# The passage from W_o to the FFN rebuilt around two cross sums, and the result of a decoder layer put together in token rows

## The chip, the cores and the metric

One core of a Trainium2 chip runs the kernel. The metric is the device time of one execution in microseconds. TensorE multiplies matrices, VectorE and ScalarE do everything element by element, GpSimd does little here, and SyncE (SP) issues most DMAs. Matrices in fp32 are multiplied as three products of high and low halves.

## The reference

One step of a decoder layer for 256 prompt tokens and 8 x 4 sample tokens, 288 in all, D = 2048, all fp32. The attention and the gated convolution ahead of it, and the caches, are not touched. What matters is this end of the layer:

```python
def _rmsnorm(x, g):
    y = x * lax.rsqrt(jnp.mean(x * x, axis=-1, keepdims=True) + RMS_EPS)
    return y * g

    m = (sigmoid(ga) * a + sigmoid(gb) * b) @ w_o
    x = x + gate1 * _rmsnorm(m, g_post1)                    # x1
    h = _rmsnorm(x, g_pre2) * (1.0 + scale2) + shift2       # h2
    g, u = jnp.split(h @ w_ffn_in, 2, axis=-1)              # 2 x 5632 columns
    f = (jax.nn.silu(g) * u) @ w_ffn_out
    return x + gate2 * _rmsnorm(f, g_post2)
```

shift, scale and gate come from silu(c) @ w_ada + b_ada, one set for the prompt and one for each of the eight sample sequences.

## The kernel before

**Layout.** Features lie on the 128 partitions and tokens in the columns: xT, r_T, a_hi, a_lo, x1A, f_T are 16 feature tiles (kt) of 288 columns, the first 256 prompt, the last 32 samples. All products put weights on the stationary side and 288 token columns on the moving side.

**Products.** A weight block of 512 x 512 (1 MB) is loaded by SP into one of four raw slots (load_w), ScalarE rounds it to w_hi (split_hi), VectorE forms w_lo (split_lo), each into one of two buffers. TensorE's product(n, ...) then does 4 output tiles (mt) x 4 feature tiles x 3 matmuls. ScalarE may overwrite a buffer when the product that used it is done, so both splits of block n+1 happen while product n runs. The order of each engine's work is written out by hand; semaphores carry the dependences (raw_turn: w_lo is made; mm_turn: groups of a product are done; bank_turn: PSUM banks are evicted; act_hi, act_lo: halves of the input are made).

**W_o stage.** Four turns (o_turn) of four products. After a turn, gated() on ScalarE squares each output tile into sq4 and evicts it times gate1·g_post1 into r_T; VectorE adds the squares (add_square) into sqr. Beside the products TensorE works through the remaining columns of w_ada in groups of 512 (ADA): four slots of fp32 matmuls (ada_slot), ScalarE copies the group (copy_ada), TensorE turns it (ada_transpose), VectorE adds the four parts (add_ada). Groups ADA_T and ADA_T + 1 are done in the passage.

**Passage.** sum_partitions adds sqr and the last square over partitions, as a product with ones into bank 7. inverse_root makes rstd with logarithm and exponential on ScalarE and one refining step in three VectorE operations (refine_root). add_normed scales r_T by rstd and adds it to xT, in 8 pieces of two tiles: xT is now x1. ScalarE squares each piece (square_x1), TensorE sums the squares over partitions, and ScalarE scales x1 into x1A (scale_x1). A second inverse_root follows, then h2 = x1A·rstd + shift2 piece by piece (h2_times_rstd, split_h2, h2_lo). TensorE meanwhile does the two ADA groups, and eight matmuls into bank 6 whose result nothing reads. The first FFN product waits for pieces 0 and 1; pieces 2 to 7 are made in the first FFN turn ahead of the product that needs them. A turn of the FFN (f1_turn) is 4 products for the gate half, then 4 for the up half.

**End.** After W_ffn_out, r and x change roles with f: root, add_normed(f_T) into xT, TensorE turns each block of four tiles and 128 tokens (12 blocks, the third of each four with 32 tokens), ScalarE copies it to y_rows (one block VectorE), and SP stores four chunks of 512 columns.

## Time and profile before

| | |
|---|---|
| median of 3 runs | 1817.82 us (1817.79 to 1817.87) |
| profiled execution | 1817.98 us |
| its span | 1816.1 us |
| TensorE busy | 1792.5 us, 99% |
| VectorE busy | 887.6 us, 49% |
| ScalarE busy | 708.4 us, 39% |
| granted TensorE clock, mean | 0.997 |

The span runs from the first to the last instruction or transfer of the profiled execution; its own time is 1.9 us longer. Busy time of TensorE counts a matmul until its modelled end. A group's idle time says what ended the wait in front of it.

### The profile page before, as it was taken

The numbers are of one execution on the slowest core, as the hardware profiler recorded it, in microseconds if no ns is written. First come the engines' busy times: TensorE is split into PE (matmuls) and PEld (weight loads), VectorE is DVE, ScalarE is ACT, GpSimd is POOL, SyncE is SP. The second block draws the span as 40 slices with busy tenths as digits, with TensorE's granted clock in tenths as the row PEclk, the third lists the DMA queues.
The fourth block names the chain that finished last, engine by engine and source line by source line (L and its number), as shares of the span: only waits on it lengthen the run. The fifth ranks groups of instructions, "written<-read, shape, count | busy, mean of one in ns | idle before, by whom it ended". The sixth has DMA issues, their size and how long they took to land.

```text
span 1816.1 us, 31913 instructions
## 1 busy us (share of the span) xinstructions
PE 1792.5 (99%) x13683; PEld 1680.2 (93%) x13683; DVE 887.6 (49%) x1092; ACT 708.4 (39%) x829; POOL 23.7 (1%) x72
## 2 busy tenths in 40 slices
PE   9999999999999999999999999999999999999997
PEld 6888888897699999998969999999999999999996
DVE  3566662335644344453475344434444445565565
ACT  4433233335643333344363323333333334545453
POOL 0000100001000000000000000000000000000000
PEclk9999999999999999999999999999999999999999
DMA  9998788966655555559837555555555445555541
GB/s 322 380 361 310 266 302 303 339 240 210 243 186 168 168 165 166 162 203 349 305 118 255 192 201 163 164 165 168 168 166 163 162 162 162 163 164 164 168 156 52
DMA packets 193897, 382.38 MB, mean 211 GB/s; under 512 B 8998, under 2 KB 17662, under 8 KB 193504
## 3 DMA queue, kind: packets, MB, share of 16 engines
q1 hardware_dynamic: 190048, 378.04, 61.0%
q0 software_dynamic: 1328, 2.58, 0.4%
q8 instruction: 74, 1.21, 0.3%
q10 hardware_dynamic: 2424, 0.37, 0.2%
q14 instruction: 23, 0.18, 0.0%
HBM read 376.15 MB, written 4.81 MB: 210 GB/s over the span
## 4 chain that ended last, share of the span: by engine, by line
PE 94%; DVE 2%; ACT 1%; DMA 1%; SPq 1%; issue 1%; DVEq 0%; ACTq 0%
PE bank L621 29%; PE bank L623 28%; PE bank L622 28%; PE bank L631 4%; DMA ada<-in_w_ada 1%; PE bank L858 1%; PE bank L988 1%; PE bank L640 1%; PE bank L957 0%; SPq L455 0%; SPq L440 0%; DVE xT L2184 0%; PE bank L927 0%; DVE f_T L2176 0%; ACT x1A L1523 0%
## 5 line engine op out<-in xcount | busy, mean ns | idle before, releaser
L621 PE MATMUL bank<-a_lo,w_hi 128*128 128x288 f32 x3648 | 1085.1, 297 | 2.9 <-DVE a_lo L2194 1.5
L622 PE MATMUL bank<-a_hi,w_hi 128*128 128x288 f32 x3648 | 1076.2, 295 | 0.0
L623 PE MATMUL bank<-a_hi,w_lo 128*128 128x288 f32 x3648 | 1072.5, 294 | 0.0
L1612 DVE TENSOR_TENSOR w_lo<-raw,w_hi 128x2048 fp32r<-128x2048 f32 x240 | 550.0, 2292 | 700.9 <-ACT w_hi L1157 700.5
L1157 ACT CAST w_hi<-raw 128x2048 fp32r<-128x2048 f32 x239 | 455.9, 1907 | 854.6 <-PE bank L623 821.9
L621 PEld LDWEIGHTS bank<-a_lo,w_hi 128*128 128x128 f32 x3648 | 683.5, 187 | 22.1 <-issue 19.2
L623 PEld LDWEIGHTS bank<-a_hi,w_lo 128*128 128x128 f32 x3648 | 687.1, 188 | 0.0
L622 PEld LDWEIGHTS bank<-a_hi,w_hi 128*128 128x128 f32 x3648 | 684.9, 188 | 0.0
L631 PE MATMUL bank<-ada,cT 128*32 128x512 f32 (+1 forms) x608 | 64.5, 564 | 1.7 <-DMA ada<-in_w_ada 1.6
L1712 DVE TENSOR_TENSOR a_lo<-hid,a_hi 128x1152 fp32r<-128x1152 f32 x44 | 59.4, 1352 | 12.3 <-ACT a_hi L1187 12.3
L1187 ACT CAST a_hi<-hid 128x1152 fp32r<-128x1152 f32 x44 | 50.7, 1154 | 0.0
L631 PEld LDWEIGHTS bank<-ada,cT 128*32 128x32 f32 x608 | 17.9, 112 | 35.2 <-issue 29.9
L1697 DVE TENSOR_REDUCE mods<-bank 128x36 f32<-128x144 f32 (+1 forms) x22 | 6.7, 306 | 74.4 <-PE bank L640 74.3
L621 PE MATMUL bank<-o_lo,w_hi 128*128 128x288 f32 x128 | 37.9, 296 | 0.0
L621 PE MATMUL bank<-y_lo,w_hi 128*128 128x288 f32 x128 | 37.9, 296 | 0.0
L622 PE MATMUL bank<-o_hi,w_hi 128*128 128x288 f32 x128 | 37.8, 295 | 0.0
L622 PE MATMUL bank<-y_hi,w_hi 128*128 128x288 f32 x128 | 37.8, 295 | 0.0
L623 PE MATMUL bank<-o_hi,w_lo 128*128 128x288 f32 x128 | 37.6, 294 | 0.0
L623 PE MATMUL bank<-y_hi,w_lo 128*128 128x288 f32 x128 | 37.6, 294 | 0.0
L1561 ACT ACTIVATE sg<-bank 128x288 f32<-128x288 f32 x44 | 18.0, 408 | 36.8 <-PE bank L623 36.8
L1183 ACT COPY ada_sb<-bank 128x512 f32<-128x512 f32 (+1 forms) x26 | 14.4, 554 | 40.2 <-PE bank L631 40.2
L2247 DVE TENSOR_TENSOR sg<-bank,sg 128x288 f32<-128x288 f32 x44 | 19.0, 452 | 15.4 <-ACT sg L1561 15.4
(298 smaller groups left out, 943.7 us busy)
## 6 DMA issues: line engine op xcount, KB each, us to landing
raw<-in_w_ffn_in SPq DMA_DIRECT2D x88, 1024.0 KB, 5.1
raw<-in_w_in SPq DMA_DIRECT2D x75, 1024.0 KB, 10.6
ada<-in_w_ada SPq DMA_DIRECT2D x60, 1024.0 KB, 9.6
raw<-in_w_ffn_out SPq DMA_DIRECT2D x44, 1024.0 KB, 5.2
ada_o<-in_w_ada SPq DMA_DIRECT2D x26, 1024.0 KB, 9.6
raw<-in_w_o SPq DMA_DIRECT2D x16, 1024.0 KB, 6.1
ada<-in_w_ada SPq DMA_DIRECT2D x16, 512.0 KB, 10.2
raw<-in_cache_k SPq DMA_DIRECT2D x16, 512.0 KB, 4.3
```

Source lines behind the costliest of these rows:

```text
L621: pe.matmul(acc, w_hi[buf][:, a, cols], lo[:, kt, :], start=first and a == 0, stop=False)
L622: pe.matmul(acc, w_hi[buf][:, a, cols], hi[:, kt, :], start=False, stop=False)
L623: mm = pe.matmul(acc, w_lo[buf][:, a, cols], hi[:, kt, :], start=False, stop=last and a == tiles - 1)
L631: mm = pe.matmul(bank[4][32 * a:32 * a + 32, 0:cols.stop - cols.start], cT[:, SK * q + a, :], ring[q % len(ring)][:, a, cols], start=q == ...
L640: mm = pe.transpose(bank[5][:, m * P:m * P + P], ada_sb[:, m * P:m * P + P], ident[:, :])
L858: mm = pe.transpose(bank[4 + n % 2][:, f * P:f * P + P], raw[2 * j][:, n, f * P:f * P + P], ident[:, :])
L988: mm = pe.matmul(acc, lhs, rhs, start=blk == 0, stop=blk == 2, tile_position=(0, 32 * c), skip_group_check=True)
L1157: nc.scalar.copy(w_hi[buf][:, :, :], raw[s][:, :, :]).then_inc(hi_done, 1)
L1187: nc.scalar.copy(dst[:, kd:kd + tiles, :], src[:, bass.ds(kt, tiles), :]).then_inc(act_hi, 1)
L1612: tt(w_lo[buf][:, :, :], raw[s][:, :, :], w_hi[buf][:, :, :].bitcast(F32), ALU.subtract).then_inc(raw_turn, 1)
L1712: tt(lo[:, kd:kd + SK, :], src[:, bass.ds(kt, SK), :], hi[:, kd:kd + SK, :].bitcast(F32), ALU.subtract).then_inc(act_lo, 1)
L2247: tt(sg[:, mt, :], bank[mt][:, 0:NT], sg[:, mt, :], ALU.mult).then_inc(bank_turn, 1)
```

## The change

- **Sums.** With r the gated output of W_o and s = rstd, x1 = x + s·r, so the sum of x1² is x·x + 2s·(x·r) + s²·(r·r). The sum of x·x is taken from the first normalisation (its sums lie in small[:, 12:15]); VectorE spreads it on three diagonals (diag2), TensorE turns it into all partitions between the mixer and the W_o stage, and VectorE keeps it as base_x. VectorE forms x·r and r·r for the tiles of the first three W_o turns in the turn behind (cross_c, cross_q, into c_sum and q_sum), and tile by tile in the last (c_last, q_last, whose prompt columns ScalarE squares). TensorE sums both over partitions in ten matmuls ahead of group ADA_T. second_root puts the three together; rstd1 is a tile of its own.
- **x1 in pieces.** Pieces 0 and 1 are made before the FFN, the other six in the first FFN turn (x1_pieces). The square sums over x1 and the eight matmuls into bank 6 are gone.
- **First FFN turn.** Gate and up halves alternate for each group of four feature tiles, in banks 0 to 3 and 4 to 7, and the first product starts with piece 0 alone. Weight block N_F1 + 1 is rounded before the second root. The sigmoids move from the fourth product to the seventh.
- **ADA slots.** Two of the four slots of group ADA_T + 1 get another place and are loaded as soon as W_o is done.
- **End.** The sums of f² are made with tokens on partitions (one column for each 128 tokens). TensorE turns x1 and the gated f block by block; ScalarE copies x1 to y_rows; VectorE adds f times its root to it, one operation for each of the 12 blocks, and writes y_rows.

```diff
+        part, k = (t % 2, t // 2) if first else (t // 4, t % 4)
+        col = part * DFF + i * SN
+        load_w(N_F1 + PER_F1 * i + t, t % RAW, wv_f1[k, :, :, bass.ds(col, SN)])
         if first and t == 3:
+            sp.wait_ge(mm_turn, MT * (SPLIT + N_F1))
             for q in range(2, SK):
-                sp.wait_ge(ada_turn, SK * (ADA_T + 1) + q + 1)
...
+pe.wait_ge(diag2_done, 1)
+for b in range(3):
+    rows = min(P, NT - b * P)
+    mm = pe.matmul(bank[7][:, b * P:b * P + rows], ones[0:rows, 0:P], diag2[0:rows, b, 0:rows],
+                   start=True, stop=True)
+mm.then_inc(base_ps, 1)
...
+evicted = BT + MT * (G_O + O_ADA + 1)
...
+pe.wait_ge(c_done, 1)
+add_sum(6, c_sum[:, :], True)
+pe.wait_ge(bank_turn, evicted + 1)
+add_sum(0, q_sum[:, :], True)
+for mt in range(MT):
+    pe.wait_ge(c_done, mt + 1)
+    add_sum(6, c_last[:, mt, :], False, mt == MT - 1)
+    pe.wait_ge(bank_turn, evicted + mt + 1)
+    add_sum(0, q_last[:, mt, :], False, mt == MT - 1)
 ada_group(ADA_T, ada_o)
-pe.wait_ge(rstd_ready, 2)
-pe.wait_ge(eps_done, 1)
-pe.matmul(bank[7][:, 0:NT], ones[:, 0:P], sqr[:, :], start=True, stop=False)
-for p in range(PIECES):
-    pe.wait_ge(sq_done, Q_X1 + p + 1)
-    for a in range(PIECE):
-        mm = pe.matmul(bank[7][:, 0:NT], ones[:, 0:P], (sq4, sq4b)[p // 2 % 2][:, PIECE * (p % 2) + a, :],
-                       start=False, stop=p == PIECES - 1 and a == PIECE - 1)
-    mm.then_inc(ms_ps, 1)
 ada_transpose(ADA_T)
 pe.wait_ge(ada_copied, ADA_T + 2)
 for q in range(SK):
     ada_slot(q, 1, ada_t, ada_t_full)
-pe.wait_ge(raw_turn, RAW + N_F1 + 1)
-for a in range(SK):
-    pe.matmul(bank[6][:, :], w_hi[0][:, a, 0:P], w_hi[0][:, a, :], start=True, stop=True)
-for a in range(SK):
-    pe.matmul(bank[6][:, 0:TP], w_hi[0][:, a, 0:P], w_hi[0][:, a, 0:TP], start=True, stop=True)
+def first_f1():
...
+    pe.wait_ge(raw_turn, RAW + N_F1 + 1)
+    for h in range(2):
+        if h == 0:
+            pe.wait_ge(h2_first, 1)
+        else:
+            pe.wait_ge(act_lo, 10 + 1)
...
+    for t in range(1, PER_F1):
+        k, part = t // 2, t % 2
+        pe.wait_ge(act_lo, 10 + k + 1)
+        product(N_F1 + t, k == 0, k == SK - 1, None, SK * k, a_hi, a_lo, t % SPLIT,
+                None, banks_free if t == 1 else None, SK, MT * part)
...
-sum_partitions(MT + 2 * LAST, Q_F + KT)
...
+def turn_out(n, src, j):
+    c, b = n // 3, n % 3
+    rows = min(P, NT - b * P)
+    for a in range(SK):
+        mm = pe.transpose(bank[Y_BANKS[n % 4][j]][0:rows, a * P:a * P + P],
+                          src[:, SK * c + a, b * P:b * P + rows], ident[:, :])
+    return mm
...
+for n in range(12):
+    if n == 1:
+        pe.wait_ge(bank_turn, BT + MT * (G_END + 1))
+        pe.wait_ge(f_gated, 1)
+    if n == 3:
+        pe.wait_ge(ms_done, 5)
+    if n >= 4:
+        pe.wait_ge(x1_rows, n - 3)
+    turn_out(n, xT, 0).then_inc(x1_ps, 1)
+    if n == 0:
+        pe.wait_ge(sqr_done, MT + 2 * LAST)
+        pe.wait_ge(sq_done, Q_F + KT)
+        for b in range(3):
+            rows = min(P, NT - b * P)
+            at_ = slice(b * P, b * P + rows)
+            pe.matmul(bank[7][0:rows, b:b + 1], sqr[:, at_], ones[:, 0:1], start=True, stop=False)
+            mm = pe.matmul(bank[7][0:rows, b:b + 1], sq4[:, MT - 1, at_], ones[:, 0:1], start=False, stop=True)
+        mm.then_inc(ms_ps, 1)
+    if n >= 4:
+        pe.wait_ge(y_out, n - 3)
+    turn_out(n, f_T, 1).then_inc(y_ps, 1)
...
+        if mt == MT - 1:
+            last()
+        nc.scalar.activation(q_last[:, mt, 0:TP], bank[mt][:, 0:TP], ACT.Square,
+                             scale=modG[:, kt, 0:1].rearrange("p a n -> p (a n)")).then_inc(bank_turn, 1)
...
+o_turn(O_ADA, None, False, lambda: inverse_root(2, M_O + 1))
...
+split_hi(N_F1 + 1, 1, R_F1 + 1, 1)
+act.wait_ge(ms_done, 3)
+nc.scalar.activation(rstd1[:, :], sq4[:, 1, :], ACT.Ln, scale=-2.0).then_inc(ms_done, 1)
+act.wait_ge(ms_done, 4)
+nc.scalar.activation(rstd1[:, :], rstd1[:, :], ACT.Exp, scale=-0.5).then_inc(root_done, 1)
+scale_x1(0)
+copy_ada(ADA_T)
 split_h2(0)
+scale_x1(1)
 split_h2(1)
...
+        if first and t == 0:
+            scale_x1(2)
+            scale_x1(3)
+            split_hi(n + 2, 2, R_F1 + 1, 0)
+            split_h2(2)
+            split_h2(3)
+        elif not (first and t == 1):
+            split_hi(n + 1, (t + 1) % RAW, R_F1 + 2 * i + (t + 1) // RAW + 1, (t + 1) % SPLIT)
...
-        if first and t < 3:
-            split_h2(2 * t + 2)
-            split_h2(2 * t + 3)
-        if t == 3:
+        if first and t in (2, 4):
+            scale_x1(t + 2)
+            scale_x1(t + 3)
+            split_h2(t + 2)
+            split_h2(t + 3)
...
+copy_x1(0)
+act.wait_ge(ms_done, 5)
+own.mark(nc.scalar.activation(roots[:, 0:3], small[:, 12:15], ACT.Ln))
+own.wait()
+nc.scalar.activation(roots[:, 0:3], roots[:, 0:3], ACT.Exp, scale=-0.5).then_inc(root_done, 1)
+for n in range(1, 12):
+    copy_x1(n)
...
+for b in range(3):
+    ins = ts(diag2[:, b, :], ident[:, :], small[:, 12 + b:13 + b], None, ALU.mult)
+ins.then_inc(diag2_done, 1)
...
+def cross_sum(c, left, right, total):
+    k = slice(SK * c, SK * c + SK)
+    own.mark(tt(sq4[:, :, :], left[:, k, :], right[:, k, :], ALU.mult))
+    own.wait()
+    own.mark(tt(sq4[:, 0:2, :], sq4[:, 0:2, :], sq4[:, 2:4, :], ALU.add))
+    own.wait()
+    if c == 0:
+        own.mark(tt(total[:, :], sq4[:, 0, :], sq4[:, 1, :], ALU.add))
+    else:
+        own.mark(tt(total[:, :], total[:, :], sq4[:, 0, :], ALU.add))
+        own.wait()
+        own.mark(tt(total[:, :], total[:, :], sq4[:, 1, :], ALU.add))
+    own.wait()
...
+def cross_c(c):
+    dve.wait_ge(sqr_done, MT + MT * (c + 1))
+    dve.wait_ge(bank_turn, BT + MT * (G_O + c + 2))
+    gate_samples(r_T, c)
+    own.wait()
+    cross_sum(c, xT, r_T, c_sum)
+def cross_q(c):
+    cross_sum(c, r_T, r_T, q_sum)
...
+        if i > 0 and t == 0:
+            cross_c(i - 1)
+        if i > 0 and t == 1:
+            cross_q(i - 1)
+        if i == O_ADA and t == 2:
+            dve.wait_ge(ada_mods, ADA_T + 1)
+            add_bias(3 * KT, 5 * KT)
+            scaled(modA, 2 * KT, 4, 1.0)
...
+for mt in range(MT):
+    kt = MT * i + mt
+    if mt < MT - 1:
+        add_square(mt, MT * i + Q_O + mt + 1, MT * i + MT + mt)
+    dve.wait_ge(r_done, mt + 1)
+    v = seqs(r_T[:, kt:kt + 1, TP:NT], 1)
+    own.mark(tt(v, v, cond(modG, kt, 1), ALU.mult))
+    own.wait()
+    own.mark(tt(q_last[:, mt, TP:NT], r_T[:, kt, TP:NT], r_T[:, kt, TP:NT], ALU.mult))
+    tt(c_last[:, mt, :], xT[:, kt, :], r_T[:, kt, :], ALU.mult).then_inc(c_done, 1)
...
+def second_root():
...
+    dve.wait_ge(cq_ps, 2)
+    own.mark(stt(sq4[:, 2, :], bank[0][:, 0:NT], -0.5 / D, rstd[:, :], ALU.mult, ALU.mult))
+    own.wait()
+    own.mark(stt(sq4[:, 2, :], bank[6][:, 0:NT], -1.0 / D, sq4[:, 2, :], ALU.mult, ALU.add))
+    own.wait()
+    own.mark(tt(sq4[:, 2, :], sq4[:, 2, :], rstd[:, :], ALU.mult))
+    own.wait()
+    own.mark(tt(sq4[:, 2, :], sq4[:, 2, :], base_x[:, :], ALU.add))
+    own.wait()
+    ts(sq4[:, 1, :], sq4[:, 2, :], -0.5 * EPS, None, ALU.min).then_inc(ms_done, 1)
+def x1_times(p):
+    v = piece(r_T, p)
+    own.mark(tt(v, v, rstd[:, :].unsqueeze(1).broadcast_to([P, PIECE, NT]), ALU.mult))
+    return own.n
+def x1_add(p, n):
+    own.wait(n)
+    tt(piece(xT, p), piece(xT, p), piece(r_T, p), ALU.add).then_inc(x1_done, 1)
...
+def x1_pieces(p):
+    first, second = x1_times(p), x1_times(p + 1)
+    x1_add(p, first)
+    x1_add(p + 1, second)
+    x1_samples(p)
+    x1_samples(p + 1)
+inverse_root(2, M_O + 1, 2)
+n = x1_times(0)
+x1_times(1)
+second_root()
+x1_add(0, n)
+x1_samples(0)
+refine_root(3, rstd1)
 def h2_times_rstd(p):
     k0 = PIECE * p
     dve.wait_ge(x1A_done, p + 1)
+    own.wait()
     v = piece(x1A, p)
-    own.mark(tt(v, v, rstd[:, :].unsqueeze(1).broadcast_to([P, PIECE, NT]), ALU.mult))
+    own.mark(tt(v, v, rstd1[:, :].unsqueeze(1).broadcast_to([P, PIECE, NT]), ALU.mult))
...
 h2_times_rstd(0)
+x1_add(1, n + 1)
+h2_lo(0)
+x1_samples(1)
+add_ada(ADA_T, ADA_T)
 h2_times_rstd(1)
-h2_lo(0)
 h2_lo(1)
-add_ada(ADA_T, ADA_T)
+own.mark(nc.vector.memset(sqr[:, :], D * EPS / P))
...
+        if ga is not None and t == (0 if first else 4):
             add_ada(ga, ga)
-        if first and t < 3:
-            h2_lo(2 * t + 2)
-            h2_lo(2 * t + 3)
+        if first and t in (0, 1, 3):
+            x1_pieces(t + 3 if t else 2)
+        if first and t in (0, 2, 4):
+            h2_times_rstd(t + 2)
+            h2_times_rstd(t + 3)
+            h2_lo(t + 2)
+            h2_lo(t + 3)
...
+dve.wait_ge(bank_turn, BT + MT * (G_END + 1))
+v = seqs(f_T[:, SK * 3:SK * 4, TP:NT], SK)
+tt(v, v, cond(modG, SK * 3, SK), ALU.mult).then_inc(f_gated, 1)
+dve.wait_ge(ms_ps, M_F + 1)
+own.mark(ts(small[:, 12:14], bank[7][:, 0:2], 1.0 / D, None, ALU.mult))
+ts(small[0:TS, 14:15], bank[7][0:TS, 2:3], 1.0 / D, None, ALU.mult).then_inc(ms_done, 1)
+dve.wait_ge(root_done, 4)
+own.wait()
+own.mark(tt(roots[:, 3:6], small[:, 12:15], roots[:, 0:3], ALU.mult))
...
+for n in range(12):
+    c, b = n // 3, n % 3
+    rows = min(P, NT - b * P)
+    y = y_rows[0:rows, b, SN * c:SN * c + SN]
+    dve.wait_ge(x1_rows, n + 1)
+    dve.wait_ge(y_ps, n + 1)
+    stt(y, bank[Y_BANKS[n % 4][1]][0:rows, :], roots[0:rows, 6 + b:7 + b], y,
+        ALU.mult, ALU.add).then_inc(y_out, 1)
...
```

## Rows read from the trace of the kernel before

**Rows 1.** Page, header and part 1: span; busy time, share and instructions.

```profile
span 1816.1 us, 31913 instructions
...
PE 1792.5 (99%) x13683; PEld 1680.2 (93%) x13683; DVE 887.6 (49%) x1092; ACT 708.4 (39%) x829; POOL 23.7 (1%) x72
```

**Rows 2.** Windows, the passage and the first FFN turn: busy time, counts, granted clock, DMA share, GB/s.

```profile
915.30:940.65 25.35, 21.16 (x117) 9.87 (x115) 19.68 (x41) 17.20 (x40) 0.00 (x0) 1.00 0.35 125
940.65:992.80 52.15, 51.98 (x388) 51.74 (x389) 32.37 (x47) 23.03 (x31) 0.00 (x0) 1.00 0.64 224
```

**Rows 3.** Timeline, passage and end of first FFN turn: start, length, engine, line.

```profile
916.02 0.75 PE L1087 MATMUL bank<-sq,ones 128*128 128x288 f32 x2
...
916.70 3.64 PE L631 MATMUL bank<-ada_o,cT 128*32 128x512 f32 x32
...
917.25 0.44 ACT L1221 ACTIVATE rstd<-rstd 128x288 f32<-128x288 f32 x1
...
917.89 0.46 DVE L1656 TENSOR_TENSOR sq<-sq,rstd 128x288 f32<-128x288 f32 x1
...
922.47 2.58 PE L1098 MATMUL bank<-sq,ones 128*128 128x288 f32 x8 [1.44 <-ACT sq L1517]
...
936.01 0.46 DVE L1660 SCALAR_TENSOR_TENSOR rstd<-sq,rstd 128x288 f32<-128x288 f32 x1
...
936.50 0.76 DVE L2215 TENSOR_TENSOR x1A<-x1A,rstd 128x576 f32<-128x576 f32 x1
...
937.55 0.91 ACT L1532 ACTIVATE a_hi<-x1A,mods 128x256 fp32r<-128x256 f32 x2 [2.72 <-DVE x1A L2218]
...
938.63 0.88 DVE L2192 SCALAR_TENSOR_TENSOR a_lo<-x1A,mods,a_hi 128x256 fp32r<-128x256 f32 x2 [0.19 <-ACT a_hi L1534]
...
940.65 0.40 PE L621 MATMUL bank<-a_lo,w_hi 128*128 128x288 f32 x1 [1.29 <-DVE a_lo L2194]
...
993.00 0.46 DVE L2254 TENSOR_TENSOR hid<-bank,sg 128x288 f32<-128x288 f32 x1 [1.02 <-PE bank L623]
```

**Rows 4.** Timeline of VectorE in two W_o turns.

```profile
838.65 2.29 DVE L1612 TENSOR_TENSOR w_lo<-raw,w_hi 128x2048 fp32r<-128x2048 f32 x1 [3.72 <-ACT w_hi L1157]
...
868.45 2.29 DVE L1612 TENSOR_TENSOR w_lo<-raw,w_hi 128x2048 fp32r<-128x2048 f32 x1 [3.78 <-ACT w_hi L1157]
```

**Rows 5.** Page, parts 5 and 6: costliest groups, DMA issues.

```profile
L1157 ACT CAST w_hi<-raw 128x2048 fp32r<-128x2048 f32 x239 | 455.9, 1907 | 854.6 <-PE bank L623 821.9
...
L1712 DVE TENSOR_TENSOR a_lo<-hid,a_hi 128x1152 fp32r<-128x1152 f32 x44 | 59.4, 1352 | 12.3 <-ACT a_hi L1187 12.3
...
ada_o<-in_w_ada SPq DMA_DIRECT2D x26, 1024.0 KB, 9.6
```

**Rows 6.** Timeline of the end.

```profile
1795.77 0.75 PE L1087 MATMUL bank<-sq,ones 128*128 128x288 f32 x2
...
1802.59 2.34 PEld L1140 LDWEIGHTS bank<-ident,xT 128*128 128x128 f32 x12 [6.53 <-DVE xT L2184]
...
1808.27 1.25 PEld L1140 LDWEIGHTS bank<-ident,xT 128*128 128x128 f32 x12 [0.81 <-DVE xT L2184]
...
1811.41 0.69 DVE L2289 COPY y_rows<-bank 128x512 f32<-128x512 f32 x1 [1.19 <-PE bank L1140]
...
1811.85 0.57 ACT L1599 COPY y_rows<-bank 32x512 f32<-32x512 f32 x1 [0.29 <-PE bank L1140]
```

**Rows 7.** One line, the weight loads of a small fp32 product.

```profile
L710 PEld LDWEIGHTS bank<-diag,ones x6: 181/188/192, 22.2 to 22.9; 128*128 128x128 f32 x4, 32*128 32x128 f32 x2
```

**Rows 8.** Windows with the granted clock, at the start and at the end.

```profile
12.40:17.70 5.30, 5.30 (x31) 3.26 (x29) 4.05 (x9) 5.24 (x5) 0.00 (x0) 1.00 1.10 336
...
18.00:20.00 2.00, 2.00 (x26) 1.23 (x28) 1.29 (x8) 0.63 (x4) 0.00 (x0) 0.67 1.06 373
...
1803.00:1805.00 2.00, 2.00 (x12) 1.74 (x10) 2.00 (x4) 0.99 (x2) 0.00 (x0) 0.50 0.00 0
...
1807.00:1809.00 2.00, 1.48 (x13) 1.09 (x11) 2.00 (x4) 1.13 (x4) 0.00 (x0) 0.94 0.78 288
```

More of the change, by code:

```diff
@@ L307, in layer @@
         r_T = place("r_T", [P, KT, NT], where=R)
-        sq4b = place("sq4b", [P, SK, NT], where=off_act + (KT - SK) * NT * 4)
+        c_last = place("c_last", [P, MT, NT], where=off_act)
+        q_last = place("q_last", [P, MT, NT], where=off_act + MT * NT * 4)
+        c_sum = place("c_sum", [P, NT], where=o_sel)
+        q_sum = place("q_sum", [P, NT], where=o_sel + NT * 4)
+        assert o_sel + 2 * NT * 4 <= o_bf
+        rstd1 = place("rstd1", [P, NT], where=o_sel)
+        roots = place("roots", [P, 12], where=o_sel + NT * 4)
+        diag2 = place("diag2", [P, 3, P], where=tail)
+        base_x = place("base_x", [P, NT], where=o_qkv + 2 * B_ACT8 + 2 * SK * SN * 4)
+        assert o_qkv + 2 * B_ACT8 + 2 * SK * SN * 4 + NT * 4 <= tail
         x1A = place("x1A", [P, KT, NT], where=off_act + KT * NT * 4)
@@ L312, in layer @@
         ada_t = [place(f"ada_t{s}", [P, SK, SN], where=o_qkv + 2 * B_ACT8 + s * SK * SN * 4) for s in range(2)]
-        ada_t += ada_o[2:4]
+        ada_t += [place(f"ada_t{2 + j}", [P, SK, SN], where=off_act + j * KT * NT * 4 + 2 * SK * NT * 4) for j in range(2)]
+        assert SK * SN * 4 <= 2 * SK * NT * 4
         assert o_qkv + 2 * B_ACT8 + 2 * SK * SN * 4 <= tail
@@ L607, in _, with product @@
         def _(pe):
-            def product(n, first, last, G, kt0, hi, lo, buf, between=None, inside=None, tiles=SK):
+            def product(n, first, last, G, kt0, hi, lo, buf, between=None, inside=None, tiles=SK, banks=0):
                 pe.wait_ge(raw_turn, RAW + n + 1)
@@ L615, in product @@
                         inside(mt)
-                    if first:
+                    if first and G is not None:
                         pe.wait_ge(bank_turn, BT + MT * G + mt + 1)
@@ L1117, in f1_products @@
                         ada_beside(ga, t, ada_o, 1)
[L1118 to L1121 removed]
+            first_f1()
             for i in range(1, 1 + F_ADA):
@@ L1478, in _, with gated @@
             mix_turn(MIXES - 1, True)
-            def gated(dst, n, i, done):
+            def gated(dst, n, i, done, cross=None, last=None):
                 for mt in range(MT):
@@ L1485, in gated @@
                         act.wait_ge(sqr_done, done + mt + 1)
+                    if cross is not None and mt == 0:
+                        act.wait_ge(cross_done, cross)
                     groups_done(n, mt)
@@ L2140, in o_turn @@
+            def o_turn(i):
                 for t in range(PER_O):
                     split_lo(N_O + PER_O * i + t + 1, (t + 1) % RAW, (t + 1) % SPLIT)
-                    if first and t == 0:
+                    if i == 0 and t == 0:
                         split_act_lo(H_HI + 2 + 3, m_T, SK * 3, a_hi, a_lo, SK * 3)
-                add_ada(ADA_MAIN + i, ADA_MAIN + i)
-                for mt in range(MT):
-                    add_square(mt, MT * i + Q_O + mt + 1, MT * i + MT + mt)
-            o_turn(0, True)
@@ L2206, in _ @@
-            for c in range(4):
-                v = seqs(x1A[:, SK * c:SK * c + SK, TP:NT], SK)
-                own.mark(tt(v, seqs(xT[:, SK * c:SK * c + SK, TP:NT], SK), cond(modA, SK * c, SK), ALU.mult))
-            inverse_root(3, M_X1 + PIECES)
-            own.wait()
+            def second_root():
[9 more added lines that the diff above has]
+                ts(sq4[:, 1, :], sq4[:, 2, :], -0.5 * EPS, None, ALU.min).then_inc(ms_done, 1)
```

179 lines of the change are left out of this document (83 added, 96 removed).

## The prediction

> **What bounds the kernel now.** I read the page first: TensorE is busy for 99% of the span [rows 1], so only stretches in which it lacks matrix work can give time back. The windows show one such stretch, 915.30 to 940.65 us, between the last W_o product and the first FFN product; the windows behind it hold the first FFN turn [rows 2]. The timeline of this stretch [rows 3] shows a chain of roots and row operations: sum and first root, x1, its squares summed over partitions, second root, h2, two pieces split into high and low halves, first product at 940.65. The second poor stretch is the end: TensorE is idle from 1796.5 until its first transpose at 1802.59 and then waits for VectorE between blocks [rows 6]. These two places are 25 us and 21 us, and the change is in both. Everything between keeps its 6.4 us per product (a product is 48 matmuls), so a gain in either place reaches the end undiminished.
>
> **Change, passage from W_o to FFN.** I place the new steps on the clock of before.
>
> First root. VectorE now puts three operations (gate 32 columns, square 32 columns, multiply 288 columns; about 0.22, 0.12 and 0.40 us from one start to the next, estimated from the 288 columns at 0.49 that dependent operations take [rows 3]) behind each of the last sums of squares. A tile then takes 1.16 us in place of 0.53, the third sum ends at 916.1 and the TensorE pair that before ended in the 916.02 row is seen at 917.35, 0.6 late. A dependent 288-column VectorE operation costs 0.49 (917.89 for the first of three, 936.01 to 936.50 for the last [rows 3]), so rstd stands at 917.89 + 0.6 + 3 x 0.49 = 919.95.
>
> Cross sums. Instead of squaring x1 after it exists, the kernel sums x·r and r·r beforehand. TensorE does ten fp32 matmuls of 288 columns from 917.1. One is 0.75 us with its drain, 0.50 without: four of them fill 2.58 us with the waits between [rows 3]. They end at 922.1 and are seen at 922.4. Second root: five dependent operations, 2.5, to 924.9; logarithm and exponential at 0.44 each, 925.85; three to refine, 927.4. Before, it stood at 936.5. From there one piece is scaled (936.50 to 937.55), its high half made (to 938.63) and its low half (half of 938.63 to 940.65): 1.05 + 1.08 + 1.0, so 930.5.
>
> TensorE's own path is longer. Behind the cross sums it has the group ADA_T, 3.64 us [rows 3], to 925.7. The copy of that group waits on ScalarE behind the exponential and two scalings: 927.2. Transposes 0.75, the other group 3.6: 931.5. The first FFN product starts then, 9.15 us before 940.65. The 17 square sums (8.5 us) and the eight filling matmuls (1.8 us) are gone; this is the room.
>
> First FFN turn. What was done ahead is now done between products. Product 0 ends at 931.5 + 6.4 + 0.45 (one transposed group) = 938.35, product 1 at 944.75. Product 2 needs pieces 2 and 3 and its weights. VectorE: the low half of piece 1 until 934.1, memset 0.2, weights 2.2, sums of the group 0.2, then four 576-column operations at 0.67 and two small ones, 3.0, to 939.8. ScalarE waits for these, scales until 940.5, makes the high weights (1.91 [rows 5]) until 942.35, and only then the high half of piece 2, 943.4. VectorE: two low halves, 945.3, low weights, 947.65. TensorE waits 2.9 us. The same account gives 0.4 us to spare before product 4 and 1 us before product 6. The turn ends at 947.65 + 6 x 6.4 = 986.05. Before, it ended at 992.8, 0.2 ahead of the 993.00 row [rows 3]. Passage and turn together give 6.75 us. The size of the wait is the least certain term: with every handover 0.05 shorter it is 2, with operations as long as their busy time (0.75 for 0.67) and one more collision it is 4.5.
>
> Hidden parts. The cross sums of the first three turns: a product over 1152 columns is 1.35 [rows 5], 576 columns 0.76, 288 columns 0.49, so 3.0 to 3.5 for the first with its gate and 3.1 for the second. VectorE's gaps there are 3.72 and 3.78, and 6.40 - 2.29 = 4.11 in the middle of a turn [rows 4]; behind them the low weights are ready some 1.7 us before TensorE wants them. I count 0, and up to 0.5 if the tight one slips. The three operations on diag2 (128 columns, under 0.49 each) lie in the same kind of gap. On TensorE three more fp32 matmuls build the sum of x squared between the stages: the same pattern as the six loads from 22.2 to 22.9 [rows 7], +0.6. DMA: two of the four ADA slots are loaded to another place, on SP's queue ahead of the fifth weight load, at 915.3. They land in 9.6 [rows 5], at 925, and are wanted at 929.7: nothing, unless they take over 14. No wait for ada_turn holds back the weight loads behind them any more; also nothing, since ScalarE doesn't want these before 955.
>
> **Change, the end.** Before: root 1797 to 1799.1, VectorE makes x pieces until 1810.2, last copy ends 1812.42, span ends 3.7 later. Now TensorE turns x1 of block 0 at once (1795.04 to 1795.5), waits for the last square until 1795.75, and does six matmuls of one column, 12 passes, each bound by a weight load of 0.14 [rows 7]: 1797.35. Then 23 further groups of four transposes. At full clock twelve loads take 1.25 us [rows 6], so a group is 0.42 and a block (x1 and f) 0.84. Block 0 is done at 1797.8, block 11 at 1807.0. VectorE: two small operations, then ScalarE's two on three columns (0.2 each), four more at 0.2: 1799.25. One operation per block, nearest row 0.69 for 512 columns from PSUM [rows 6], 0.75 with the scalar: faster than TensorE's 0.84, so it catches up and ends at 1807.85. ScalarE's copies (0.57) hide behind the same 0.84. With the same 3.7 to the end of the store: 1811.55, 4.55 less than 1816.1.
>
> **Sum.** The profiled execution took 1817.98 (span 1816.1), 0.16 over the median. 1817.98 - 6.75 + 0.6 - 4.55 = 1807.3.
>
> **Clock.** In the end stretch the granted clock was 0.50 (1.2 GHz) at 1803 to 1805, after 6 us of idle TensorE, and back to 0.94 in 1807 to 1809, though in between only transposes ran [rows 8]; twelve loads took 2.34 at half clock, 1.25 at full [rows 6]. At the kernel's start the opposite: from 12.40 to 17.70 TensorE only turned x, at full clock, and at 18 to 20 the clock was 0.67 [rows 8]. The new end is nothing but transposes for 11 us, denser than those of the start (31 in 5.3 us there).
>
> The Trainium skill, TensorE: Matmul & The Clock Gate, Part 4: PE-mode transpose, says that transposes don't count as busy for the clock. The start agrees, the rise at 1807 doesn't. By that rule the tail would run at half clock to its end, which is the third case below; by the rise at 1807 the sum stands. I take the rise, since it is the same instruction in the same place.
>
> **Rivals.** *The clock dips once at the end.* The idle 0.25 us and the one-column matmuls are thin work. Half clock for some 4.5 us, as before from 1802.6 to 1807, costs half of it: 2.3, 1809.6. For it: the start. Against: dense transposes raised the clock.
>
> *Transposes don't hold the clock.* From about 1801 on, where some four blocks of eleven are done, the other seven take 1.7 each in place of 0.84: 6 later, 1813.3; if it falls at 1799, 1815.7.
>
> *The first turn waits more.* If the wait ahead of product 2 grows to 5, and the 0.4 and 1.0 us of slack ahead of products 4 and 6 are lost by 1 us each, or the clock dips in the wait: 4 later, 1811.3. For it: that turn is a chain through two engines with ScalarE behind VectorE behind ScalarE. Against: the waits of one engine for the other are already in the account.
>
> *Slower than before.* The same handovers, the three places alike: past the slack each further microsecond counts three times. The gain of 10.7 is gone at about 4 us more in each of the three, and over 0.2% slower from 5 us. Nothing in the rows is that long except two weight splits falling into the chain.
>
> *The cross sums don't move the root.* If the second root's chain, not TensorE's groups, starts the FFN, nothing changes until it is 1 us later than computed; then one for one.
>
> **How the numbers follow.** Forecast 0.52; one dip 0.18; more waiting in the first turn 0.14; no clock for transposes 0.09; slower 0.04; other small ones around no change 0.03. What a measurement here can tell from no change is 0.2%, 3.6 us: faster is below 1814.2. The first three cases lie there, and two thirds of the fourth: 0.90; same 0.06; slower 0.04. The range takes the wait at 2 us and the tail at its best (1805.5) up to the third case with some of its bound (1811.8).
>
> **What would show it.** First FFN matmul 25.35 - 9.15 = 16.2 us behind the last of W_o; one TensorE wait near 3 us ahead of the third product and none over 0.5 behind it; no new wait in the W_o turns; clock 1.00 in all 2 us windows of the end; twelve VectorE operations of 0.7 to 0.75 ending 13 us after the last product; TensorE's busy time lower in the passage, since 27 matmuls fewer stand against ten more. I am wrong if the clock falls while transposes run, if VectorE, not TensorE, paces the end, or if products 4 and 6 wait too.

## The result, and the profile after

The changed kernel takes 1808.49 us (median of 5, 1808.07 to 1809.72) against 1817.82 us of the kernel before beside it: ratio 0.9947, 95% interval 0.9935 to 0.996. That is faster, by 9.3 us at the medians. Forecast were 1807.3 us and a range of 1805.5 to 1811.8. The profiled execution is the slowest of the five, 1809.72 us, with a span of 1808.1; a second set of five executions of the same kernel gave 1807.63 us and a profile with a span of 1805.8.

The page of the profile, header and part 1, answers to [rows 1]: 2.5 us less of TensorE's busy time in a span 8.0 us shorter.

```profile
span 1808.1 us, 32032 instructions
...
PE 1790.0 (99%) x13723; PEld 1683.2 (93%) x13723; DVE 905.5 (50%) x1134; ACT 705.4 (39%) x826; POOL 23.7 (1%) x72
```

To see where the 8.0 us come from I cut the span at two instructions that both kernels have: the last matmul of W_o and the last of all products. Timeline of the kernel before (start, length, engine, line):

```profile
915.17 0.29 PE L623 MATMUL bank<-a_hi,w_lo 128*128 128x288 f32 x1
...
1794.91 0.29 PE L623 MATMUL bank<-a_hi,w_lo 128*128 128x288 f32 x1
```

Timeline of the kernel after, from the same matmul on:

```profile
917.00 0.29 PE L637 MATMUL bank<-a_hi,w_lo 128*128 128x288 f32 x1
917.85 0.75 PE L1107 MATMUL bank<-sqr,ones 128*128 128x288 f32 x2 [0.55 <-DVE sqr L2217]
...
923.28 0.65 PE L1116 MATMUL bank<-q_last,ones 128*128 128x288 f32 x2
923.86 3.64 PE L645 MATMUL bank<-ada_o,cT 128*32 128x512 f32 x32
928.52 0.66 PE L654 MATMUL bank<-ident,ada_sb 128*128 128x128 f32 x4 [1.02 <-ACT ada_sb L1253]
929.11 3.64 PE L645 MATMUL bank<-ada_t,cT 128*32 128x512 f32 x32
932.68 0.40 PE L1155 MATMUL bank<-a_lo,w_hi 128*128 128x288 f32 x1
...
948.80 0.43 PE L635 MATMUL bank<-a_lo,w_hi 128*128 128x288 f32 x1 [2.63 <-DVE w_lo L1696]
...
1656.76 0.37 PE L635 MATMUL bank<-a_lo,w_hi 128*128 128x288 f32 x1 [0.17 <-DVE w_lo L1696]
...
1791.20 0.29 PE L637 MATMUL bank<-a_hi,w_lo 128*128 128x288 f32 x1
```

| stretch | before | after | difference | forecast |
|---|---|---|---|---|
| start to last W_o matmul | 915.17 | 917.00 | +1.83 | +0.6 |
| last W_o matmul to last product matmul | 879.74 | 874.20 | -5.54 | -6.75 |
| last product matmul to the end | 21.19 | 16.90 | -4.29 | -4.55 |
| span | 1816.1 | 1808.1 | -8.0 | -10.7 |

The first row of the table isn't the change's main work. Of its 1.83 us, the three matmuls for the sum of x squared are 0.7; the rest is accounted for by TensorE's waits for the first blocks of w_ada, which are 2.9 us in total in this profile and 1.6 in that of the kernel before.

The first FFN matmul stands 15.68 us behind the last of W_o; before it was 25.5 [rows 3]. One wait is longer than half a microsecond in the whole turn behind it: 2.63 us, before the third product, for w_lo. What the table doesn't show is what follows this wait. Windows of 2 us (busy time and count of TensorE, its weight loads, VectorE, ScalarE, GpSimd; granted clock; DMA share; GB/s), kernel after:

```profile
946.00:948.00 2.00, 0.17 (x2) 0.00 (x0) 2.00 (x3) 1.74 (x1) 0.00 (x0) 1.00 0.00 0
948.00:950.00 2.00, 1.20 (x6) 1.23 (x7) 2.00 (x4) 0.16 (x1) 0.00 (x0) 0.74 0.13 20
950.00:952.00 2.00, 2.00 (x10) 2.00 (x10) 2.00 (x5) 1.31 (x4) 0.00 (x0) 0.50 0.97 332
952.00:954.00 2.00, 2.00 (x16) 2.00 (x16) 2.00 (x2) 0.40 (x2) 0.00 (x0) 0.91 0.49 180
954.00:956.00 2.00, 2.00 (x18) 2.00 (x17) 1.75 (x5) 1.24 (x4) 0.00 (x0) 1.00 0.51 110
```

TensorE idles from 946.2, and from 949.0 to 952.4 its clock is at half, 1.2 GHz: 10 matmuls in a window where there are 17 or 18 at full clock. The idle itself is read from the waits; that the work behind it also ran slower is seen only in the clock column.

The end, timeline of TensorE and VectorE, answers to [rows 6]:

```profile
1791.34 0.60 PE L1189 MATMUL bank<-ident,xT 128*128 128x128 f32 x4
1792.15 0.35 PE L1208 MATMUL bank<-ones,sqr 128*128 128x1 f32 x2 [0.21 <-ACT sq L1560]
...
1793.32 0.66 PE L1189 MATMUL bank<-ident,f_T 128*128 128x128 f32 x4
1793.81 0.60 PE L1189 MATMUL bank<-ident,xT 128*128 128x128 f32 x4
...
1802.98 0.60 PE L1189 MATMUL bank<-ident,f_T 128*32 128x128 f32 x4
```

```profile
1794.94 9.59 DVE L2472 SCALAR_TENSOR_TENSOR y_rows<-bank,roots,y_rows 128x512 f32<-128x512 f32 x12
```

From 1793.32 on TensorE turns one group each 0.437 us without a gap, and VectorE's twelve operations follow it to 1804.53. The clock in this stretch, which answers to [rows 8]:

```profile
1796.00:1798.00 2.00, 2.00 (x21) 1.92 (x20) 1.97 (x4) 1.23 (x3) 0.00 (x0) 1.00 0.03 10
1798.00:1800.00 2.00, 2.00 (x21) 1.98 (x19) 1.75 (x3) 1.41 (x3) 0.00 (x0) 1.00 0.81 293
1800.00:1802.00 2.00, 2.00 (x21) 1.91 (x19) 1.67 (x3) 1.41 (x3) 0.00 (x0) 1.00 0.80 287
1802.00:1804.00 2.00, 1.58 (x15) 1.21 (x13) 1.71 (x3) 1.18 (x3) 0.00 (x0) 1.00 0.59 230
```

### The profile page after: what moved, and what is told of

The parts are those of the page before. It is cut to its first block, busy times and chain, and to the rows that moved or that the text cites. A ratio compares the mean times of both kernels' runs of the same rounds, so it can differ in the third digit from the quotient of the medians.

```text
span 1808.1 us, 32032 instructions
## 1 busy us (share of the span) xinstructions
PE 1790.0 (99%) x13723; PEld 1683.2 (93%) x13723; DVE 905.5 (50%) x1134; ACT 705.4 (39%) x826; POOL 23.7 (1%) x72
## 4 chain that ended last, share of the span: by engine, by line
PE 94%; DVE 2%; DMA 1%; ACT 1%; SPq 1%; issue 1%; DVEq 0%; ACTq 0%
PE bank L635 29%; PE bank L637 28%; PE bank L636 28%; PE bank L645 4%; DMA ada<-in_w_ada 1%; PE bank L872 1%; PE bank L1002 1%; PE bank L1189 1%; PE bank L654 0%; PE bank L971 0%; SPq L470 0%; ACT w_hi L1227 0%; SPq L455 0%; DVE w_lo L1696 0%; PE bank L941 0%
## 5 line engine op out<-in xcount | busy, mean ns | idle before, releaser
L1781 DVE TENSOR_REDUCE mods<-bank 128x36 f32<-128x144 f32 x22 | 6.7, 305 | 73.5 <-PE bank L654 73.5
```

## The experiments

Two questions. Which part earns what, and are the two gains independent? And what ties the FFN's first turn: is the wait before product 2 what it seems, does it bring the fall of the clock with it, and can both be had back? The table gives for each kernel the time beside the kernel before (which had a median of 1818.27, 1817.89 and 1818.29 us in the three sets), and from its profile the stretch between the last W_o matmul and the last product matmul ("middle"), that from there to the end ("end"), and the waits of over 2 us or those that took their place. The start-up is left out of both stretches: the last W_o matmul came between 914.76 and 917.01 us in the kernels after and its variants, whose work up to there is nearly the same. Two things differ there from profile to profile: the waits for the first ADA weights, 1.2 to 3.2 us in total, and the granted clock, which was at half for some 3.4 us within the first 24 us in four of these eleven profiles (the first of the kernel after, wait filled, and both with a start at piece 1) and at 1.00 in the others. So a difference of about 2 us between two times is read from the stretches, not from the times.

| kernel | us | ratio, 95% interval | middle | end | wait before product 2, clock behind it |
|---|---|---|---|---|---|
| before | | | 879.74 | 21.19 | none |
| after | 1808.49 | 0.9947, 0.9935 to 0.996 | 874.20 | 16.90 | 2.63, fell |
| after, second time | 1807.63 | 0.9952, 0.9938 to 0.9965 | 874.21 | 16.83 | 2.64, fell |
| new end only | 1813.6 | 0.9975, 0.9965 to 0.9985 | 879.75 | 16.82 | none |
| new passage only | 1812.36 | 0.9971, 0.9959 to 0.9984 | 872.66 | 21.19 | 2.63, 1.00 |
| wait filled | 1807.44 | 0.9941, 0.9927 to 0.9954 | 872.68 | 16.81 | 0.36, 1.00 |
| order of w_lo | 1806.42 | 0.9933, 0.992 to 0.9947 | 871.65 | 16.78 | 1.57, 1.00 |
| order and gaps | 1804.97 | 0.9928, 0.9915 to 0.9942 | 870.33 | 16.85 | 0.26, 1.00 |
| best | 1804.1 | 0.9931, 0.9917 to 0.9944 | 869.85 | 16.87 | 0.25, 1.00 |
| best, start at piece 1 | 1808.2 | 0.9942, 0.9928 to 0.9955 | 872.45 | 16.83 | none; 2.81 before product 0, 1.00 |
| after, start at piece 1 | 1812.65 | 0.9962, 0.9948 to 0.9976 | 879.53 | 16.85 | 2.38, fell; 2.81 before product 0, fell |
| longer wait | 1812.24 | 0.9966, 0.9954 to 0.9978 | 878.14 | 16.81 | 5.42, fell |
| x1 turned twice | 1812.6 | 0.997, 0.9959 to 0.9981 | 874.21 | 21.66 | 2.64, fell |
| before, end kept busy | 1817.84 | 1.0, 0.9991 to 1.001 | 879.78 | 21.09 | none |

**New end only.** The kernel before with the whole end of the kernel after (both sides as in the change's diff).

```diff
-sum_partitions(MT + 2 * LAST, Q_F + KT)
+for n in range(12):
+    turn_out(n, xT, 0).then_inc(x1_ps, 1)
...
+    turn_out(n, f_T, 1).then_inc(y_ps, 1)
```

> The kernel before with the new end alone (x1 and gated f turned block by block, one VectorE operation per block, sums of f squared in columns). Theory: the two parts of the change are independent and the end gives 4.0 us of it (17.0 us from the last product to the end of the span in place of 21.1), so 1813.8 us, and the granted clock stays 1.00 through all the transposes. Rival, the end gains only because the passage left something ready: then less than 2 us, over 1815.8. Rival, the clock falls among the transposes here: blocks of 1.7 us in the trace and no gain.

Measured 1813.6 us, 4.7 under the kernel before; the end takes 16.82 in place of 21.19, the middle is the same to 0.01.

**New passage only.** The kernel after with the old end.

```diff
-for n in range(12):
-    turn_out(n, xT, 0).then_inc(x1_ps, 1)
...
-    turn_out(n, f_T, 1).then_inc(y_ps, 1)
+sum_partitions(MT + 2 * LAST, Q_F + KT)
```

> The changed kernel with the old end put back. Theory: cross sums, pieces and the alternating first FFN turn give 5.8 us from the last W_o product to the second FFN turn, less 0.6 for the three matmuls for x squared: 1812.6 us. The trace should show again one TensorE wait of 2.6 us ahead of product 2 and the clock at 0.50 for some 3.4 us after it. Rival, the parts share a gain: the sum of this kernel's gain and that of the new end alone would differ from 9.3 us by more than 1.

Measured 1812.36 us, 5.9 under the kernel before; the end is the old one, 21.19. At the medians the two parts gain 10.6 us, 1.3 more than the 9.3 of the whole, so the limit of 1 that was set for the rival is passed. The stretches show no shared gain, though: the end is worth 4.4 us alone and 4.3 in the kernel after, and the middle differs from that of the kernel after by the clock alone. The parts add up, 4.4 us at the end and 5.5 to 7.1 in the middle. The expected fall of the clock did not come. The profile has the same 2.63 us wait, and no fall of the clock (windows of this kernel):

```profile
946.00:948.00 2.00, 0.45 (x3) 0.48 (x4) 2.00 (x3) 0.91 (x1) 0.00 (x0) 1.00 0.00 0
948.00:950.00 2.00, 2.00 (x17) 2.00 (x16) 2.00 (x5) 0.56 (x2) 0.00 (x0) 1.00 0.69 174
950.00:952.00 2.00, 2.00 (x17) 2.00 (x16) 2.00 (x4) 1.15 (x3) 0.00 (x0) 1.00 0.93 358
```

The middle is 1.54 us shorter than in the kernel after, 872.66 for 874.20, with the same instructions and the same wait in it. This is what the fall costs in these two profiles.

**Wait filled.** Six fp32 matmuls of 224 columns, whose result nothing reads, in the wait before product 2.

```diff
+if t == 2:
+    for _ in range(FILL):
+        pe.matmul(bank[6][:, NT:SN], ones[:, 0:P], ones[:, 0:SN - NT], start=False, stop=False)
 pe.wait_ge(act_lo, 10 + k + 1)
```

> The changed kernel with six fp32 matmuls of 224 columns (about 0.39 us each, 2.3 us together, result read by nothing) in TensorE's wait ahead of product 2 of the first FFN turn. Theory: the clock falls because TensorE is idle there for 2.6 us, and that fall costs half of 3.4 us. With the wait filled the clock stays 1.00, the rest of the turn is 1.7 us shorter, and the time is 1.5 to 1.9 us below the changed kernel (about 1806.6). Rival, the fall comes from the thin passage ahead of it (two waits of TensorE for the cross sums and the copied group): the clock falls all the same and the time is unchanged or up to 0.5 us longer.

The clock was 1.00 in the whole turn and the middle 872.68, that of the new passage without the fall. This one profile doesn't prove that the filling kept the clock up, since the new passage alone kept it with the wait unfilled. Taken with the next three variants it is likely: none of the four profiles with this wait at 1.57 us or less has the fall. The time, 1807.44 us, is 0.2 to 1.05 under the two medians of the kernel after and misses the 1.5 to 1.9 of the theory. That would fit a fall in most executions and not in all, but the start-up moves by more.

**The unchanged kernel again.** No edit.

> The changed kernel once more, unaltered. In its first profile the wait of 2.6 us ahead of product 2 was followed by 3.4 us at half clock; in the kernel with the old end put back the same wait was followed by none. Theory: the same wait leads to the fall in some executions and not in others, so the times of this kernel spread by up to 1.7 us more than those of a kernel without the wait, and its median lies between. Expected 1807.5 to 1809.5, with either clock in the profile. Rival, the fall belongs to every execution of this kernel: the profile shows it again and the lowest time is no lower than 1808.

Middle and end agree with the first profile to 0.07 us each, and the clock fell again. The two spans differ by 2.3, and the last W_o matmul stands at 917.00 in the one and at 914.76 in the other: all of the difference lies ahead of the change's main parts. Half of it is the waits for ADA weights, 2.9 against 1.8 us. The first profile also has a fall of the clock at the start, from 10.3 to 13.7 us, which the second lacks; it can make up the rest. The five times, 1806.62 to 1812.07 us, settle neither theory nor rival: the lowest is below the rival's 1808, and the spread of 5.5 is far more than a fall of 1.5 can make.

**Order of w_lo.** The wait is for w_lo of product 2. Timeline of VectorE in the kernel after, ahead of it:

```profile
941.95 0.75 DVE L2376 TENSOR_TENSOR x1A<-x1A,rstd 128x576 f32<-128x576 f32 x1
942.74 0.22 DVE L2379 TENSOR_TENSOR x1A<-x1A,mods 128x64 f32<-128x64 f32 x1
944.49 0.88 DVE L2318 SCALAR_TENSOR_TENSOR a_lo<-x1A,mods,a_hi 128x256 fp32r<-128x256 f32 x2 [1.53 <-ACT a_hi L1604]
...
946.24 0.22 DVE L2320 TENSOR_TENSOR a_lo<-x1A,a_hi 128x64 fp32r<-128x64 f32 x1
946.37 2.28 DVE L1696 TENSOR_TENSOR w_lo<-raw,w_hi 128x2048 fp32r<-128x2048 f32 x1
```

VectorE idles for 1.53 us, waiting for the high half of piece 2, while w_hi of product 2 has been there since 943.5 (ScalarE makes it first). With w_lo moved ahead of the low halves, most of this gap is used:

```diff
+if not (first and t == 1):
+    split_lo(n + 1, (t + 1) % RAW, (t + 1) % SPLIT)
-split_lo(n + 1, (t + 1) % RAW, (t + 1) % SPLIT)
...
 h2_times_rstd(t + 3)
+if t == 0:
+    split_lo(n + 2, 2, 0)
 h2_lo(t + 2)
```

> The kernel after with one edit only: the low weights of product 2 are made ahead of the low halves of pieces 2 and 3. Theory: the wait before product 2 shrinks from 2.6 to between 1.2 and 1.9 us, the clock does not fall behind it, and the time is 0.9 us shorter for the wait and 1 to 1.7 us for the clock: 1805.2 to 1807.2. Rival (the late low halves of pieces 2 and 3 hold up products 4 and 6 instead): a wait of over 0.5 us appears at one of them and the time is within 0.6 us of the kernel after.

As the theory had it: the wait is 1.57 us and now for a_lo, the clock stays, the middle is 2.55 shorter (1.06 of it the wait, the rest the clock), the time 1806.42 us. No wait came up at products 4 and 6.

**Order and gaps.** In addition the r times rstd of pieces 2 and 3 are made in two gaps of VectorE, ahead of the second root and ahead of the low half of piece 1.

```diff
 x1_times(1)
+made2 = x1_times(2)
 second_root()
...
 h2_times_rstd(1)
+made3 = x1_times(3)
 h2_lo(1)
...
-x1_pieces(t + 3 if t else 2)
+x1_pieces(t + 3 if t else 2, None if t else (made2, made3))
```

> The changed kernel with three VectorE steps put elsewhere: the low weights of product 2 are made ahead of the low halves of pieces 2 and 3 (in the 1.5 us in which VectorE waits for ScalarE), and r times rstd of pieces 2 and 3 in the gaps ahead of the second root and ahead of piece 1's low half. Theory, VectorE's queue bounds the start of product 2: the wait of 2.6 us shrinks by 0.95 + 1.3 to 0.4 us, no fall of the clock follows, and the time is 3.5 to 4 us below the changed kernel (about 1804.7). Rival, the chain through ScalarE bounds it (scaling, high weights, high half): the wait shrinks by under 1 us, to 1.7 or more.

The time is 1804.97 us. The wait is 0.26 us: VectorE's chain has been nearly the whole of it.

**Best.** In addition, in the last W_o turn, the squares 0 and 1 are added together ahead of tile 0's row operations, and square 2 one tile later.

```diff
-if mt < MT - 1:
-    add_square(mt, MT * i + Q_O + mt + 1, MT * i + MT + mt)
+for s in ((0, 1), (2,), (), ())[mt]:
+    add_square(s, MT * i + Q_O + s + 1, MT * i + MT + s)
```

> The kernel with the three VectorE steps moved, and the sums of squares of the last W_o turn put ahead of the new multiplications (the first two sums together, the third behind one tile's multiplications). TensorE waited 0.55 us for the third sum, and everything behind it follows. Theory: that wait goes and the time falls by 0.4 to 0.6 us against the kernel with the three steps moved (1804.4). Rival, the multiplications that are now later hold up the cross sums: TensorE waits for c_last or q_last instead and nothing is gained.

TensorE's 0.55 us wait for sqr ahead of the passage is gone and the middle 0.48 shorter. At 1804.1 us (five executions, 1803.82 to 1808.03) this is the fastest version, 3.5 to 4.4 us under the kernel after at the medians; in the middle it is 4.35 shorter.

**After, start at piece 1.** Is the early start with piece 0 alone worth its code, if product 2 waits anyway?

```diff
 pe.wait_ge(h2_first, 1)
+pe.wait_ge(act_lo, 10 + 1)
```

> The kernel after, with the FFN's first product waiting for piece 1 of the input as well, so that it starts about 2.6 us later instead of at the end of piece 0's low half. Theory (what bounds the passage up to product 2 is VectorE's chain of low halves and low weights, and the half start only moves the wait): the wait before product 2 shrinks from 2.6 us to under 1, the granted clock stays at 1.00 behind it, and the time is within 1.2 us of the kernel after, 1806.8 to 1809.2. Rival (VectorE and ScalarE follow product 0, so the whole chain shifts): the wait stays at 2 us or more and the time is 2.2 to 2.8 us longer, 1810.2 or more.

My theory fell. The wait before product 2 stayed at 2.38 us, and the time went up by 4.2 to 5.0. The timeline of VectorE in this kernel says why:

```profile
933.85 2.22 DVE L1697 TENSOR_TENSOR w_lo<-raw,w_hi 128x2048 fp32r<-128x2048 f32 x1
941.32 0.31 DVE L1782 TENSOR_REDUCE mods<-bank 128x36 f32<-128x144 f32 x1 [5.25 <-PE bank L654]
941.55 1.42 DVE L2343 TENSOR_TENSOR r_T<-r_T,rstd 128x576 f32<-128x576 f32 x2
```

VectorE idles for 5.25 us at the reduction of the ADA group. Its transposes stand in TensorE's order behind the first half of product 0; so what VectorE does for pieces 2 and 3 can't begin before that half is done, and a late product 0 moves everything behind it. In the kernel after this wait is nil: the transposes are done at 937.4, VectorE comes to the reduction at 937.67. What was on record as rival was right, except that the loss is larger than its 2.8. The middle is 5.33 longer than in the kernel after; 2.87 of it is the later start of product 0, and most of the rest is a fall that the kernel after doesn't have. Around the end of the 2.81 us wait before product 0 the clock went to half and stayed there from 933.2 to 940.0, 6.8 us; behind the 2.38 us wait it fell once more, for 3.4. Two of the five executions, 1810.54 and 1810.65 us, had a mean granted clock of 0.999, which leaves no room for the long fall (an estimate: 6.8 us at half are 0.0019 of the mean, and the second fall 0.0009); they are in the rival's range. The other three, 1812.65 to 1813.28, had 0.996 and 0.997.

**Best, start at piece 1.** The same edit in the best version.

> The version with the low weights of product 2 made ahead of the low halves of pieces 2 and 3 and the last sums of squares paired (1804.1 us), with the first product waiting for piece 1 as well. There VectorE no longer bounds product 2, so the late start is not given back. Theory: 1.5 to 2.7 us longer, about 1806.2. Rival (the half start is worth nothing there either): within 0.6 us, 1804.7 or less.

The middle is 2.60 us longer than in the best version, near the upper end of the theory's range, with no fall in the turn. The median time, 1808.2 us, is 4.1 longer and outside of that range. The five executions were 1806.78 twice and 1808.20 to 1808.46 three times: two groups apart by about the 1.5 us of a fall. That it was a fall in the three is argued, not shown; their mean clocks, 0.998, 0.998 and 0.999 against 0.999 twice, don't settle it.

**Longer wait.** The kernel after with two additions of 1152 columns on VectorE ahead of w_lo of product 2.

```diff
+if first and t == 1:
+    for _ in range(2):
+        own.mark(tt(sq4[:, :, :], sq4[:, :, :], sq4[:, :, :], ALU.add))
+        own.wait()
 split_lo(n + 1, (t + 1) % RAW, (t + 1) % SPLIT)
```

> The kernel after with two extra VectorE operations of 1152 columns, about 1.35 us each, ahead of the low weights of product 2. Theory: the wait before product 2 grows from 2.6 to about 5.3 us and the granted clock falls to 0.50 behind it: 2.7 us for the wait and up to 1 us for the fall, 1810.3 to 1812.3 against 1807.6 to 1808.5 for the kernel after. Rival one (the fall of the clock comes from something else than this wait): the fall is absent or no longer than the 3.4 us at half clock that the shorter wait left, and the time is 2.7 us longer and no more. Rival two (slack behind product 2 takes part of it): under 2 us longer.

The wait is 5.42 us, 2.79 more, and the middle 3.94 longer than in the kernel after, 5.48 longer than without a fall. The surplus of 2.7 is the clock, which was at half from 949.4 to 956.2, the last 0.8 us of the wait and 6 of work. The time, 1812.24 us, is at the upper end of the theory's range.

**x1 turned twice.** Each x1 block is turned a second time into the same bank.

```diff
+turn_out(n, xT, 0)
 turn_out(n, xT, 0).then_inc(x1_ps, 1)
```

> The changed kernel with each of the twelve x1 blocks turned twice (48 more transposes). Theory: TensorE paces the new end, at 0.44 us for four transposes, and transposes keep the clock at 1.00: 5.2 us longer than the changed kernel, 1813.7. Rival, VectorE paces it (0.80 a block): under 4 us longer. Rival, transposes don't hold the clock and the new end was only too short to show it: 0.50 in the last windows, and over 8 us longer.

The end is 21.66 us, 4.8 longer: 12 groups at 0.437 are 5.2, less what stood in a wait. TensorE paces the new end. The clock was 1.00 in each window of 2 us from 1792 to 1810, and from 1792.36 to TensorE's end at 1807.42 nothing but transposes ran. This kernel also shows that one and the same kernel runs with the fall behind product 2's wait and without it. The profiled execution has it, at a mean granted clock of 0.999; three of the seven have 1.000, which leaves at most 1.8 us at half clock (worked out from the rounding) where the fall takes 3.4.

**Before, end kept busy.** The kernel before with twelve fp32 matmuls of 288 columns while the last root is made.

```diff
 sum_partitions(MT + 2 * LAST, Q_F + KT)
+for _ in range(12):
+    pe.matmul(bank[6][:, 0:NT], ones[:, 0:P], sqr[:, :], start=True, stop=True)
```

> The kernel before with twelve fp32 matmuls of 288 columns (6 us, result read by nothing) in TensorE's wait for the last root. In the kernel before the clock was 0.50 while the first six blocks were turned. Theory: VectorE's 16 operations on x pieces set the pace of the old end, the clock doesn't, so the blocks are turned faster but the time stays within 0.3 us of the kernel before. Rival, a good part of the new end's gain is that the clock stays up: then this kernel gains over 1 us.

The clock was 1.00 at the end, where it had been 0.50 before [rows 8], and the end was no shorter than by 0.1 us. What the change saves there is VectorE's rows, not the clock: twelve operations, one each 0.80 us, take the place of 16 of 576 columns, one each 0.67 us, which with a smaller one between filled the time from 1799.11 to 1810.2.

## Why the prediction was right, point by point

**First root.** I counted 0.6 us of delay for TensorE's sum, and 0.5 came. The sum is two pairs of matmuls, over sqr and over the last square. Timeline of the kernel before, then of the kernel after:

```profile
915.30 0.65 PE L1085 MATMUL bank<-sqr,ones 128*128 128x288 f32 x2
...
916.81 0.41 ACT L1219 ACTIVATE rstd<-bank 128x288 f32<-128x288 f32 x1 [0.40 <-PE bank L1087]
```

```profile
918.43 0.65 PE L1109 MATMUL bank<-sq,ones 128*128 128x288 f32 x2
...
919.12 0.41 ACT L1289 ACTIVATE rstd<-bank 128x288 f32<-128x288 f32 x1 [0.88 <-PE bank L1109]
```

Before, the first pair did not wait for sqr; after, it waits 0.55 us, and ScalarE starts the root 2.12 us behind the last W_o matmul in place of 1.64. In the best version, where this wait is gone, it is 1.65 again. The root was done 4.64 us behind that matmul (counted 4.78).

**Cross sums.** Ten matmuls at 0.485 (counted 0.50), seen by VectorE 7.0 us behind the last W_o matmul (counted 7.2). The second root was done at 11.7 (counted 12.2), piece 0's low half at 14.9 (15.3).

**TensorE's own path** sets the first FFN product, as counted: the wait ahead of it is nil, the one for ada_sb is 1.02. It came 15.68 us behind the last W_o matmul, 0.5 earlier than the 16.2 forecast. The case that the second root's chain, not TensorE's groups, starts the FFN did not occur. TensorE lost 25 matmuls of before in the passage, 17 and 8; the 27 in the list of signs is a slip.

**The first turn.** Counted one wait of 2.9 us before product 2, for w_lo, behind a chain of VectorE and ScalarE, and none before products 4 and 6: measured 2.63 and none. The runs on order and on order and gaps show that the chain is what I described; its slack was VectorE's 1.53 us for a_hi. Passage and turn without the fall of the clock give 879.74 - 872.66 = 7.1 us, where the sum had 6.75. A new wait of 0.17 us at 1656.76 was not foreseen, and its cause was not looked for.

**The clock in this wait** is the term that the sum lacked. I had named it inside a rival ("or the clock dips in the wait") and priced it only together with other losses. It costs 1.54 us where it comes, by the two profiles whose middle differs in it alone. With it the gain is 5.5.

**The end.** Counted 4.55, measured 4.29 to 4.37. The one-column sums took 1.15 us for twelve passes, 0.10 each and not 0.14, so the root came 0.6 earlier; but a block takes 0.873 us and not 0.84 on TensorE, the spacing of its groups being 0.437. TensorE paces, as counted; VectorE's operations are 0.73 to 0.75 long, as counted, and 0.80 with their waits. One copy of ScalarE is not hidden, the last: the chain that ends last goes from the last block of x1 over its copy (0.58 us, from 1803.18) to VectorE's last operation at 1803.79.

**The clock at the end** stayed at 1.00; of the two rivals about it neither came. The rise that I had read from [rows 8] was the better guide than the kernel's start. The start was weak evidence: in eight of the fourteen profiles the same transposes at the start are followed by no fall at all.

The Trainium skill, TensorE: Matmul & The Clock Gate, Part 4: PE-mode transpose, says that transposes don't count as busy. By it the end would have run mostly at half clock; this case's runs disagree, with 1.00 through 10 us of transposes in the kernel after and through 15 us with x1 turned twice.

**Base.** Six loads and products in 0.94 us with their drain, 0.7 without (counted 0.6). The other 1.1 us by which the last W_o matmul came later belong to the start-up, and the sum had no term for it.

**The sum.** From 1807.3: +1.5 for the clock, +0.3 for the end, -0.35 for passage and turn gives 1808.7; the medians were 1808.49 and 1807.63. The start-up, which moved by 2.2 us from one profile to the next, is as large as all of these, so that the medians lie this close to 1808.7 is in part luck.

## What to carry to other kernels

When a phase ends in a chain over three engines, cost what follows it too: here the early start was worth its full time only because the next turn's chain moved with it, and the largest cheap gain (2.55 of the 4.35 us that all reorderings gave in the middle) lay in one VectorE gap behind an operation that did not need to come first. A wait on TensorE of 2.5 us in the midst of dense work can have two prices, its length and the slower work behind it, and the second is seen only in the clock column. Before an engine is blamed in a tail, give it what it is said to lack: twelve matmuls whose result nothing reads showed in one run that the old end was not held by the clock.
